# Softmax sums of the second attention one iteration later, residual steps every four ticks, and the opening's low parts on VectorE

## The reference

```
hs = concat([meta, x])                       # 16 + 512 tokens
for layer in range(2):
    h = rms_norm_2(hs, norm_mix_pre[layer])
    mix = pool_mixer(h, ...) if layer == 0 else sliding_window_attention(h, k_blk, v_blk, ...)
    hs = hs + rms_norm_2(mix, norm_mix_post[layer])
    h = rms_norm_2(hs, norm_ffn_pre[layer])
    hs = hs + rms_norm_2(swiglu(h, w_gate_up[layer], w_down[layer]), norm_ffn_post[layer])
    if layer == 0: k, v = (rms_norm_2(hs, kv_norm) @ w_k + b_k), (... @ w_v + b_v)
# attention: 16 query heads of 64, 2 kv heads; a block of 128 queries sees 256 keys
    m = max(logits.max(-1), sink); p = exp(logits - m)
    denom = p.sum(-1) + exp(sink - m); o = (p / denom) @ v
```

## Time and profile before

| | |
|---|---|
| Median of 3 executions | 2049.62 us (2049.09 to 2052.73) |
| The profiled execution, its own time | 2052.12 us |
| Its span | 2050.3 us |
| PE busy | 1909.2 us (93%) |
| DVE busy | 952.0 us (46%) |
| ACT busy | 649.9 us (32%) |
| POOL busy | 190.0 us (9%) |
| Mean granted TensorE clock | 0.967 of full speed |

### The profile page before, as it was taken

How to read it: one execution, slowest core, us unless ns; L and a number is a source line. 1 busy time by engine, 2 the same in 40 slices (tenths; PEclk the granted TensorE clock), 3 DMA queues, 4 the chain that set the end, 5 groups by cost and what they waited for, 6 DMA issues and landing times.

```text
span 2050.3 us, 30975 instructions
## 1 busy us (share of the span) xinstructions
PE 1909.2 (93%) x13274; PEld 1576.3 (77%) x13274; DVE 952.0 (46%) x1649; ACT 649.9 (32%) x1199; POOL 190.0 (9%) x173
## 2 busy tenths in 40 slices
PE   7999999979998998999799999998888879999998
PEld 5776688866665665668689999997766778888888
DVE  5655334233332332347973323357766574422345
ACT  6343323220110000045432222234455543222242
POOL 0011100110000000000300000014122420000001
PEclk9999999979999999999899999999999979999999
DMA  4222242579999999942112332343211334233343
GB/s 181 83 71 64 75 175 93 199 300 424 426 426 427 426 426 426 427 191 86 60 43 83 94 101 75 94 133 123 84 52 42 94 101 135 92 103 88 92 120 123
DMA packets 57053, 351.44 MB, mean 171 GB/s; under 512 B 7328, under 2 KB 7968, under 8 KB 44624
## 3 DMA queue, kind: packets, MB, share of 16 engines
q1 hardware_dynamic: 53088, 340.44, 44.8%
q0 software_dynamic: 3504, 8.54, 1.2%
q10 hardware_dynamic: 320, 0.43, 0.1%
HBM read 349.38 MB, written 4.19 MB: 172 GB/s over the span
## 4 chain that ended last, share of the span: by engine, by line
PE 75%; DVE 10%; DMA 8%; ACT 4%; issue 2%; POOL 1%; DVEq 0%; SPq 0%; ACTq 0%; POOLq 0%
PE bank L429 52%; PE bank L634 8%; DMA e<-in_we 7%; PE bank L656 4%; ACT SS L2512 1%; PE bank L667 1%; PE bank L477 1%; PE bank L668 1%; PE bank L783 1%; DVE wlo L1157 1%; DVE SS L1903 1%; DVE sm L1910 1%; PE bank L621 1%; POOL zacc L2608 1%; PE bank L494 1%
## 5 line engine op out<-in xcount | busy, mean ns | idle before, releaser
L429 PE MATMUL bank<-nhi,whi 128*128 128x256 f32 (+2 forms) x1184 | 375.8, 317 | 3.7 <-DVE yT L1955 1.6
L429 PE MATMUL bank<-nlo,whi 128*128 128x256 f32 (+2 forms) x1184 | 372.9, 315 | 0.0
L429 PE MATMUL bank<-nhi,wlo 128*128 128x256 f32 (+2 forms) x1184 | 372.8, 315 | 0.0
L1157 DVE TENSOR_TENSOR wlo<-raw,whi 128x1024 fp32r<-128x1024 f32 x242 | 303.3, 1258 | 130.9 <-ACT whi L2030 127.1
L2030 ACT CAST whi<-raw 128x1024 fp32r<-128x1024 f32 x247 | 257.0, 1043 | 119.7 <-PE bank L429 96.5
L429 PEld LDWEIGHTS bank<-nhi,whi 128*128 128x128 f32 x1184 | 225.4, 190 | 21.6 <-DVE nlo L1751 2.2
L634 PE MATMUL bank<-e,xT 128*64 128x256 f32 x2048 | 237.0, 385 | 0.8 <-DVE xT L1422 0.8
L429 PEld LDWEIGHTS bank<-nlo,whi 128*128 128x128 f32 x1184 | 225.0, 190 | 13.6
L429 PEld LDWEIGHTS bank<-nhi,wlo 128*128 128x128 f32 x1184 | 224.8, 190 | 13.6
L634 PEld LDWEIGHTS bank<-e,xT 128*64 128x64 f32 x2048 | 143.2, 138 | 82.5 <-issue 14.9
L429 PE MATMUL bank<-ghi,whi 128*128 128x272 f32 (+2 forms) x608 | 184.7, 304 | 9.6 <-DVE wlo L1157 9.6
(11 more groups left out here) (352 smaller groups left out, 2951.4 us busy)
## 6 DMA issues: line engine op xcount, KB each, us to landing
e<-in_we SPq DMA_DIRECT2D x96, 2048.0 KB, 33.0
raw<-in_w_down SPq DMA_DIRECT2D x64, 512.0 KB, 3.6
raw<-in_w_gate SPq DMA_DIRECT2D x48, 512.0 KB, 3.6
raw<-in_w_up SPq DMA_DIRECT2D x48, 512.0 KB, 3.6
raw<-in_w_q SPq DMA_DIRECT2D x12, 512.0 KB, 4.7
B<-in_rel POOLq DMA_DIRECT2D x8, 512.0 KB, 4.6
raw<-in_w_gc SPq DMA_DIRECT2D x8, 512.0 KB, 3.6
raw<-in_w_ga SPq DMA_DIRECT2D x8, 512.0 KB, 4.1
```

What stands on the lines that cost most here:

```text
L429: i = e.matmul(o, a, x[:, k0 + k, c0:c1], start=(k == 0 and n == 0), stop=(k == j.K - 1 and n == 2))
L1157: e.tensor_tensor(wlo[wslot(u)][:], raw[u % NRAW][:], whi[wslot(u)][:].bitcast(F32), ALU.subtract).then_inc(*hit("dve_low", ("lo", u)))
```

## The change

**Opening.** `LO_POOL` goes. The eight low parts of U_FFN to U_FFN+7 are made by DVE: two beside the products of the mixer's gate, one after each of the first two slices of `mixed_post(0)`, two behind it, two behind the pooling windows. The root of `pre0`, second range, is made by DVE too (eleven operations more), and ACT's `mean` and POOL's `root_of` go.

**Residual steps.** The steps of (fo0, 0) come every four ticks on all engines, and `KV_LAG` becomes (4, 8).

**Second attention.** PE computes scores of i ahead of the transposes of i-2. An iteration has three ticks, and each group starts two ticks later. DVE's sum and reciprocal of i-1 stand behind the maximum of i. POOL issues the bias loads at i = 5 and 9.

```diff
-            yield from nothing(11)
+            yield from nothing(11 * STEP.get((nm, r), 1))
...
         def pe_attention2():
             for i in range(18):
-                if i >= 2:      # transposes of i-2: moved behind the scores
...
+                    if t == 0:
+                        yield from nothing(2)
...
-                yield
+                yield from nothing(2)
...
-    LO_POOL = [1, *range(U_FFN, U_FFN + 8)]
-    KV_LAG = (34, 8)
+    KV_LAG = (4, 8)
+    STEP = {("fo0", 0): 4}
...
-                if u in LO_POOL:
+                if u == 1:
...
         def dve_pool():
+            root_now("pre0", 1)
             root_now("mp0", 0)
...
         def dve_open():
-            feed(U_FFN + 7)
             mixed_post(0)
+            feed(U_FFN + 5)
             windows(1, 0)
             windows(1, 1)
             windows(1, 2)
+            feed(U_FFN + 7)
             scaled_products(1, 3)
...
+                if r == 0 and s == 0:
+                    feed(U_FFN + 2)
...
+                if r == 0 and s == 1:
+                    feed(U_FFN + 3)
...
-                yield
+                yield from nothing(STEP.get((nm, r), 1))     # dve_post, act_post, pool_post
...
-                    w.wait_ge(*at("exp2", i))
+                if 1 <= i < 17:
+                    es, dn_, rc_ = (sm[:, j, 4 * i - 4:4 * i] for j in (1, 3, 4))
+                    w.wait_ge(*at("exp2", i - 1))
                     e.tensor_tensor(dn_, dn_, es, ALU.add).then_inc(*hit("dve_attn"))
                     w.wait_ge(*last("dve_attn"))
-                    e.reciprocal(rc_, dn_).then_inc(*hit("dve_attn", ("rsum2", i)))
-                yield
+                    e.reciprocal(rc_, dn_).then_inc(*hit("dve_attn", ("rsum2", i - 1)))
+                yield from nothing(2)
...
-                if i % 4 == 0 and i >= 8:
-                    pool_bias2(i // 4)
+                if i in (5, 9):
+                    pool_bias2(i // 4 + 1)
...
-        for u in LO_POOL[1:]:
-            if u == U_FFN + 2:
-                root_of("pre0", 1)
-            low(u)
```

More of the change, by code:

```diff
@@ L939, in pe_attention2 @@
             for i in range(18):
-                if i >= 2:
[L941 to L951, removed]
                 if i < 16:
@@ L968, in pe_attention2 @@
                     p.then_inc(*hit("pe_attn", ("scores2", i)))
-                yield
+                if i >= 2:
+                    g, t = (i - 2) // 4, (i - 2) % 4
+                    X = SS[(i - 2) % 4]
+                    kp, s0 = (MT, 112) if t == 0 else (128, 0)
+                    w.wait_ge(*at("normed2", i - 2))
+                    for hp in range(2):
+                        b = take(("pt2", i - 2, hp), SIDE)
+                        for x in range(2):
+                            h = 2 * hp + x
+                            e.transpose(b[0:kp, x * 256:x * 256 + 128], X[:, h, s0:128], ident)
+                            p = e.transpose(b[:, x * 256 + 128:x * 256 + 256], X[:, h, 128:256], ident)
+                        p.then_inc(*hit("pe_attn", ("turned p3", i - 2, hp)))
+                yield from nothing(2)
                 if i >= 2:
@@ L984, in pe_attention2 @@
                     p.then_inc(*hit("pe_attn", ("pv2", i - 2)))
-                    yield
+                yield
         def pe_attn2():
@@ L1906, in dve_attention2 @@
                                 *hit("dve_attn", ("free", "sc2", i, par)))
-                    mx, es, ng, dn_, rc_ = (sm[:, j, 4 * i:4 * i + 4] for j in range(5))
+                    mx, es, ng = (sm[:, j, 4 * i:4 * i + 4] for j in range(3))
                     sk = row("sinks", 4 * g, 4 * g + 4)
@@ L2280, in act_gate_step @@
                 square("pre0", r, k, hT)
-        def mean(nm, r):
-            n = quarter(nm, r)
-            w.wait_ge(*at("col", nm, r))
-            e.activation(rr[:, r, 1, 0:n], bk("col", nm, r, n=n), ACT.Identity, bias=epst[:, 0:1], scale=1.0 / D).then_inc(
-                *hit("act_mean", ("mean", nm, r), ("free", "col", nm, r)))
         def sigmoid(m, r):
@@ L2325, in act_pool @@
         def act_pool():
-            mean("pre0", 1)
             pooled_squares(0, (4, 5))
@@ L2384, in post_steps @@
                     square(nev, r, k, hT)
-                yield
+                yield from nothing(STEP.get((nm, r), 1))
         def rb_copy(nm, r):
@@ L2487, in act_attention2 @@
             for i in range(18):
+                if i < 16:
+                    while walked[0] < 2 * (i // 4) + 2:
+                        yield
+                    if i % 4 == 0:
+                        yield from nothing(2)
                 if i >= 2:
@@ L2503, in act_attention2 @@
                 if i < 16:
-                    g, t = i // 4, i % 4
-                    while walked[0] < 2 * g + 2:
-                        yield
+                    t = i % 4
                     c0 = 112 if t == 0 else 0
@@ L2757, in gpsimd @@
             w.wait_ge(marks.sem(x), 1)
-        def root_of(nm, r):
-            n = quarter(nm, r)
-            y, xm, u = (rr[:, r, i, 0:n] for i in range(3))
-            w.wait_ge(*at("mean", nm, r))
-            e.tensor_scalar(y.bitcast(I32), xm.bitcast(I32), -0.5, 1597463007.0, ALU.mult, ALU.add).then_inc(*hit("pool_root"))
-            for n in range(3):
-                w.wait_ge(*last("pool_root"))
-                e.tensor_tensor(u, y, y, ALU.mult).then_inc(*hit("pool_root"))
-                w.wait_ge(*last("pool_root"))
-                e.tensor_tensor(u, u, xm, ALU.mult).then_inc(*hit("pool_root"))
-                w.wait_ge(*last("pool_root"))
-                e.tensor_scalar(u, u, -0.5, 1.5, ALU.mult, ALU.add).then_inc(*hit("pool_root"))
-                w.wait_ge(*last("pool_root"))
-                e.tensor_tensor(y, y, u, ALU.mult).then_inc(*hit("pool_root", *([("root", nm, r)] if n == 2 else [])))
-        for u in LO_POOL[1:]:
-            if u == U_FFN + 2:
-                root_of("pre0", 1)
-            low(u)
         pool_ffn(0, pool_after0)
```

7 lines of the change are left out of this document (4 added, 3 removed).

## The result

The changed kernel took 2030.49 us in the median of four executions (2028.38 to 2032.28) beside 2051.01 for the kernel before: a ratio of 0.9897 with a 95% interval of 0.9884 to 0.991, so 21 us less (18 to 24). A second measurement beside other kernels gave 0.9905 (0.989 to 0.992). The forecast was 26 us less, 2023.3. The direction and the range held, and so did most of the mechanism of the first and third terms; the second term was far too large.

What follows compares the result with a forecast made beforehand. TensorE (PE), busy 93% of the span, was taken as the bound. The terms -5.3 - 9 - 12 = -26.3 us gave 2025.8 from the profiled 2052.12, or 2023.3 from the median 2049.62; range 2010 to 2040.

Steps and rivals of the forecast that it cites:

- first and third terms: Opening: collisions of VectorE with GpSimd given back, -5.3 us; attention: TensorE's waits shrink through the ticks, -12 us.
- second term: Residual steps: the 9.56 us wait for a low part and the half clock after it mostly go, -9 us.
- the likeliest case: Whole kernel: all three terms come as summed, 2023 us, own range 2016 to 2031; chance 0.59.
- the rival with VectorE too full: Opening and residual steps: low parts on VectorE only move the stalls; -12 us, 2037.7; chance 0.20.
- its own bound of -4: Residual steps: the smallest gain allowed, -4 us, if VectorE's collisions with POOL stay as dense as they are.
- part (2) of what would show it: Residual steps: no TensorE idle time over 3 us and clock above 0.95; a row of 5 us would refute -9.
- upper bound of 11.8: Residual steps: the most that can be had, 11.8 us, with no waits and no half clock left.
- The loop: Attention: VectorE and ScalarE take turns, period 5.75 us an iteration, which makes a group 26.15 us.
- the title's edit: Attention: VectorE's sum and reciprocal of i-1 behind the maximum of i, worth under 0.1 us an iteration by itself.
- TensorE alone as bound: Rival for all three stages: TensorE's waits go whole, 37.1 us less, 2012.5; chance 0.12.
- the slow rival: Attention: transposes wait for POOL's normalised block and hold up the scores, making the kernel slower, 2054; chance 0.05.

Runs made afterwards that it cites:

- e1_opening: Only the opening's edits (low parts and root of pre0 on VectorE) put on the kernel before; ratio 0.9969, 6.4 us.
- o1_root_only: Kernel before with only the root of pre0's second range moved to VectorE, low parts left on GpSimd; one profile, opening stretch 112.33 us (before 111.86).
- r2_pool_short: Changed kernel with GpSimd's two kinds of additions in fo0's residual steps cut to one column; one profile, stretch 47.03 us, 7.8 us shorter.

## Why the prediction was right, and where it was not

**Direction and size.** 26.3 us were forecast for the profiled execution, its like stretches gave 17.3, the timed ratio 21 (18 to 24). On average over all profiles the three stretches are shorter by 6.3, 2.8 and 12.9 us, 22 together, which fits the timed ratio: in the single pair of profiles the attention's part came out small. The miss is in the residual steps, by 6 us; the other two terms gave 1 us more each. That the time lies in the range says little of the mechanism: 2030.49 is as far from the likeliest case, 2023.3, as from the rival with VectorE too full, 2037.7. Only the stages tell the two apart: the opening and the attention go with the likeliest case, the residual steps with the rival.

**Opening, -5.3, measured -6.4.** The mechanism (collisions given back against low parts and a root added) is shown by `e1_opening`, and `o1_root_only` shows that it needs the low parts. TensorE started 6.6 us earlier relative to the first broadcast (7.0 forecast; the prediction's own terms, 9.2 - 4.1 + 1.13, make 6.2 and not 5.9, so 6.7) and waited 0.78 at the zn, not 2: the step that was off is how much of VectorE's idle time fills up. The Trainium skill's advice for a saturated VectorE ("Perfetto Trace Analysis", Optimizing Scalar/DVE Operations), that giving work away may make sense, did not carry over to this stage: VectorE is busy 36.50 of 40.00 us there with the work taken back, and the stage is 6.4 us shorter. The same section's caution, that between VectorE and GpSimd it might not help, fits. The Trainium skill's "SBUF — State Buffer" (Who interferes with whom) calls the port pair of the two engines an exclusive lock; 2.47 us beside 0.44 for the same add agree with it.

**Residual steps, -9, measured -2.05 in the changed kernel's profile, and -3.8 in the two that lost least to the clock.** This is the step that failed, beyond its own bound of -4. The prediction wrote "I leave 2 to 3 us of waits", and 3.9 us were left: off by 1 to 2. What was not in the sum is that even waits so short are followed by matmuls at half clock: it counted the 2.2 us that the clock costs before (1.6 by the rows, as half clock ended at 1418.66) as regained, with the long stall gone. Instead 1.7 to 5.1 us were lost after. The stretch's idle time fell by 5.6 us, its busy time rose by 3.5. The condition in part (2) of what would show it, no idle time over 3 us, was met, the clock above 0.95 was not (0.91), and the prediction named both of its ways to be wrong here: low parts that find VectorE behind, and a clock that falls at an unforeseen stall. The forecast's cause for the remaining wait, VectorE's total with collisions, is shown by `r2_pool_short` and by VectorE's rows; its upper bound of 11.8 was sound, since that kernel reaches 9.85.

**Attention, -12, measured -8.8 in one pair of profiles, -12.9 over all, -12.5 timed alone.** The sum is near, its make-up is not, and that is luck in part: idle time of TensorE fell by 6.3 us where 9.7 were counted (15.1 less 5.4), and the clock gave back the rest, on average more than the 2.3 counted. The loop was read rightly: a period without a tile's end is 5.84 (5.75 forecast), the wait of the sum moved to `nlo` at its full length, 34.3 us in 16 times before and 36.9 in 16 after, and taking `nlo` out broke it. Group length was 26.85, forecast 26.15. Wrong was the sentence that "the gain comes from the ticks" and that the title's edit is worth under 0.1 us an iteration: lost clock apart, leaving out the edit costs 2 us of 7, as much as leaving out the ticks, and with the clock 7.0 us in the one profile. Its worth lies where a tile ends inside an iteration, which a steady iteration doesn't show.

**The rivals.** TensorE alone as bound did not come true in any stage; VectorE too full is what the residual steps look like, and only they. POOL's late normalised block, which the prediction had "in time", costs TensorE 4.5 us in four waits, half of the 9.2 us that it still idles in the attention: the slow rival's place was real, its size a sixth of the 26.3 us that it would have needed.

**What stays open** is when the clock falls after a wait of one to three microseconds. With equal instructions it fell once or twice in the residual steps, and took 3.4 to 13.4 us of the attention of before.

## What to carry to other kernels

An operation moved off a busy engine onto one that shares its port can cost the busy engine more than doing it itself: look for rows of an operation that take five times as long as their like, and at who runs beside them. When a stall shrinks, sum the busy time of the matmul engine too, for short waits can bring slow matmuls in their place; and take more than one profile before a stage's gain is read from a pair, since the same instructions lost 3 or 13 us to the clock here. A wait is worth moving behind other work only where other work stands behind it: look at the iterations that hold something extra, not at the steady one.

## What the hardware showed that was not expected

After idle times of 2.64 and 1.22 us, with TensorE nearly always busy before, the granted clock was at its lower level (1.2 GHz, half) for 3.4 and 6.8 us. Before the change a single wait of 9.56 us cost only 1.6 us of matmul work, since 7.0 of its 10.2 us at half clock fell into the wait itself. After waits of 1.40 and 0.87 us in the attention's later groups it stayed at full speed; with the attention of before it fell after waits of 2.48 us in some groups and not in others.
